# Latent attention of one layer with its up-projections moved from the keys and values to the queries and the outputs, in a two-block transformer kernel

## The reference

```python
c_kv = _rmsnorm(kv_raw, kv_norm_g)                      # (256 tokens, 256 latents)
q_lat = jnp.einsum('bqhd,hdc->bqhc', qb, w_uk)          # queries (head dim 128) into the latent space
logits = jnp.einsum('bqhc,bqkc->bqhk', q_lat, kv_sel) * DSA_HEAD_DIM ** -0.5   # minus slope * distance
p = jax.nn.softmax(logits, axis=-1)
o_lat = jnp.einsum('bqhk,bqkc->bqhc', p, kv_sel)
o = jnp.einsum('bqhc,hcd->bqhd', o_lat, w_uv)           # back to head dim 128
```

## Time and profile before

| what | value |
|---|---|
| median of 3 runs | 1394.24 us (1393.57 to 1398.60) |
| time of the profiled execution | 1398.6 us, its span 1396.9 us |
| mean granted TensorE clock | 0.978 of full |
| busy, share of the span | TensorE 88%, weight loads 66%, VectorE 77%, ScalarE 44%, GpSimd 21% |
| transfers | 416.63 MB, mean 298 GB/s |

### The profile page before, as it was taken

One profiled execution on the slowest core, in us unless ns is written; L12 is line 12 of the kernel. 1 busy time (PEld: TensorE's weight loads), 2 busy tenths in 40 slices (PEclk: granted clock), 3 DMA queues, 4 the chain that ended last, 5 costly groups with the idle time before them and its releaser, 6 DMA issues. The chain is left out here.

```text
span 1396.9 us, 19581 instructions
## 1 busy us (share of the span) xinstructions
PE 1233.3 (88%) x6990; PEld 923.0 (66%) x6990; DVE 1070.5 (77%) x2160; ACT 613.9 (44%) x1260; POOL 288.4 (21%) x278
## 2 busy tenths in 40 slices
PE   4999999998988877777877877778899999999998
PEld 3999999998933322333333322333599989999997
DVE  6897668778888777776777777776698968998656
ACT  4576365546244333233333333233553255554445
POOL 1000000001345534444444434442000000000000
PEclk8999999999999999999999999999999999999999
DMA  9946535554989999999999999999753444554460
GB/s 393 370 168 246 211 106 198 210 182 155 411 352 427 428 427 427 427 428 427 428 427 426 428 428 427 427 428 427 301 188 133 146 175 181 182 189 165 169 230 34
DMA packets 54911, 416.63 MB, mean 298 GB/s; under 512 B 6049, under 2 KB 6689, under 8 KB 8370
## 3 DMA queue, kind: packets, MB, share of 16 engines
q0 software_dynamic: 36864, 268.45, 45.7%
q1 hardware_dynamic: 17648, 146.78, 28.7%
q10 hardware_dynamic: 322, 0.36, 0.1%
HBM read 414.52 MB, written 1.05 MB: 298 GB/s over the span
## 5 line engine op out<-in xcount | busy, mean ns | idle before, releaser
L997 PE MATMUL ps<-arena 128*128 128x512 f32 x512 | 237.5, 610 | 63.1 <-ACT arena L1453 63.1
L997 PE MATMUL ps<-ring,arena 128*128 128x512 f32 x444 | 215.6, 637 | 46.0 <-ACT arena L1453 43.9
L997 PEld LDWEIGHTS ps<-arena 128*128 128x128 f32 x512 | 94.1, 192 | 204.5 <-ACT arena L1453 103.2
L2066 DVE CUSTOM_DVE_ANT_0 arena<-arena 128x1024 f32<-128x1024 f32 x128 | 151.9, 1224 | 100.5 <-DMA arena<-in_experts,rowid 95.6
L596 POOL DMA_INDIRECT arena<-in_experts,rowid x128 | 131.1, 1024 | 363.9 <-DVE rowid L2043 198.3
L997 PEld LDWEIGHTS ps<-ring,arena 128*128 128x128 f32 x444 | 87.8, 204 | 171.8 <-issue 98.9
L673 PE MATMUL ps<-h_hi,w_lo 128*128 128x256 f32 x704 | 197.3, 280 | 0.0
L672 PE MATMUL ps<-h_hi,w_hi 128*128 128x256 f32 x672 | 189.4, 282 | 1.0 <-DVE xT L2345 0.9
L1446 ACT ACTIVATE arena<-arena 128x2 f32<-128x2 f32 x126 | 25.6, 203 | 373.2 <-DVE arena L2066 373.0
L674 PE MATMUL ps<-h_lo,w_hi 128*128 128x256 f32 x672 | 187.8, 280 | 0.0
L596 POOL DMA_INDIRECT ring<-in_experts,rowid x112 | 130.5, 1165 | 140.4 <-PE ps L997 90.3
(11 more groups left out here) (362 smaller groups left out, 2532.0 us busy)
## 6 DMA issues: line engine op xcount, KB each, us to landing
ring<-in_early_w SPq DMA_DIRECT2D x47, 1024.0 KB, 4.9
arena<-in_ada_w SPq DMA_DIRECT2D x24, 1024.0 KB, 7.3
arena<-in_up_w SPq DMA_DIRECT2D x11, 2048.0 KB, 7.7
arena<-in_z_w SPq DMA_DIRECT2D x8, 2048.0 KB, 7.9
arena<-in_down_w SPq DMA_DIRECT2D x8, 1408.0 KB, 5.9
arena<-in_o_w SPq DMA_DIRECT2D x2, 2048.0 KB, 7.7
arena<-in_pg_w SPq DMA_DIRECT2D x2, 2048.0 KB, 8.3
arena<-in_experts,rowid POOLq DMA_INDIRECT x128
```

Of the source, the lines that this page charges most:

```text
L997: mm = pe.matmul(BK[4 + 2 * t + b], diag[:, j, :], rows[j][:, D + b * 512:D + (b + 1) * 512], start=first and j == 0, stop=last and j == ( ...
L2066: v.tensor_tensor_reduce(out=u, in0=u, in1=h2tok[:, t, :], scale=1.0, scalar=0.0, op0=ALU.mult, op1=ALU.add, accum_out=dots[:, even, j:j + ...
```

## The change

The weights w_uk are applied to the queries and w_uv to the mixed latents, as the reference's own lines have it. For each head TensorE now computes `head_query(h)` (two matmuls of 256 columns into BK[4], copied by ScalarE to qlat), `head_logits(h)` against the shared latents kvT with a contraction of 256 instead of 128, `head_mix(h)` against the latents for both halves of the 256 latent features (BK[7], copied by ScalarE to olat), and `head_out(h)` with w_uv into BK[6]. The mix needs the latents with tokens on the partitions: four transposes behind block gq 0, and a copy on VectorE (ckv_tok, 512 more values per partition). w_uk now comes in its given layout, in runs of 1 KB, instead of a host-made layout with 8 KB a partition.

```diff
                 if key == ("dq", 1):
                     sp.wait_ge(S("n1_ss"), KD)
-                    sp.dma_start(wuk, w["wuk_t"]).then_inc(S("dsa_in"), 16)
+                    sp.dma_start(wuk.rearrange("p a b -> p (a b)").rearrange("p (h c) -> p h c", c=LAT),
+                                 w["dsa_w_uk"][0].rearrange("h d c -> d h c")).then_inc(S("dsa_in"), 16)
...
             for b in range(4):
                 plain("gq", b)
+                if b == 0:
+                    pe.wait_ge(S("kv_h"), 1)
+                    for t in range(NT):
+                        for i in range(2):
+                            mm = pe.transpose(BK[7][:, t * LAT + i * P:t * LAT + (i + 1) * P],
+                                              kvT[:, i, t * P:(t + 1) * P], ident[:, :])
+                    mm.then_inc(S("ckv_mm"), 1)
...
             pe.wait_ge(S("gla_in"), 1)
+            pe.wait_ge(S("ckv_tok"), 1)
...
-            def head_kv(h):
-                for b in range(2):
-                    pe.matmul(BK[4][:, 0:T], wuk_h[:, h, b, :], kvT[:, b, :], start=b == 0, stop=b == 1)
-                for t in range(NT):
-                    for b in range(2):
-                        mm = pe.matmul(BK[4][:, T + t * P:T + (t + 1) * P], kvT[:, b, t * P:(t + 1) * P],
-                                       wuv[:, h, b, :], start=b == 0, stop=b == 1)
-                mm.then_inc(S("headkv_mm"), 1)
+            def head_query(h):
+                for b in range(2):
+                    mm = pe.matmul(BK[4][:, b * T:(b + 1) * T], wuk_h[:, h, b * P:(b + 1) * P], dqT[:, h, :],
+                                   start=True, stop=True)
+                mm.then_inc(S("qlat_mm"), 1)
             def head_logits(h):
-                pe.wait_ge(S("headkv"), h + 1)
+                pe.wait_ge(S("qlat"), h + 1)
                 for t in range(NT):
-                    mm = pe.matmul(BK[5][:, t * P:t * P + P * (t + 1)], dqT[:, h, t * P:(t + 1) * P],
-                                   headkv[:, h % 2, 0:P * (t + 1)], start=True, stop=True)
+                    for b in range(2):
+                        mm = pe.matmul(BK[5][:, t * P:t * P + P * (t + 1)], qlat[:, b, t * P:(t + 1) * P],
+                                       kvT[:, b, 0:P * (t + 1)], start=b == 0, stop=b == 1)
                 mm.then_inc(S("logit_mm"), 1)
             def head_turn(h):
                 pe.wait_ge(S("p_ready"), h + 1)
+                if h:
+                    pe.wait_ge(S("dsa_cp"), h)
...
             def head_mix(h):
                 pe.wait_ge(S("pT"), h + 1)
-                if h:
-                    pe.wait_ge(S("dsa_cp"), h)
-                for t in range(NT):
-                    for kt in range(t + 1):
-                        mm = pe.matmul(BK[7][:, t * P:(t + 1) * P],
-                                       headkv[:, h % 2, T + kt * P:T + (kt + 1) * P], pT[:, t + kt, :],
-                                       start=kt == 0, stop=kt == t)
+                for b in range(2):
+                    for t in range(NT):
+                        for kt in range(t + 1):
+                            mm = pe.matmul(BK[7][:, b * T + t * P:b * T + (t + 1) * P],
+                                           ckv_tok[:, kt, b * P:(b + 1) * P], pT[:, t + kt, :],
+                                           start=kt == 0, stop=kt == t)
+                mm.then_inc(S("olat_mm"), 1)
+            def head_out(h):
+                pe.wait_ge(S("olat"), h + 1)
+                for b in range(2):
+                    mm = pe.matmul(BK[6][:, 0:T], wuv[:, h, b, :], olat[:, b, :], start=b == 0, stop=b == 1)
                 mm.then_inc(S("dsa_mm"), 1)
...
-            head_kv(0)
+            head_query(0)
             for h in range(AH):
...
+                if h:
+                    head_out(h - 1)
                 if h + 1 < AH:
-                    head_kv(h + 1)
+                    head_query(h + 1)
                 plain(name, 2 * h % 8 + 1)
...
                 if b == 0:
                     head_mix(AH - 1)
+                if b == 1:
+                    head_out(AH - 1)
...
 -            def copy_kv(h):
-                act.wait_ge(S("headkv_mm"), h + 1)
-                act.activation(headkv[:, h % 2, :], BK[4], ACT.Copy).then_inc(S("headkv"), 1)
-            copy_kv(0)
+            def query(h):
+                act.wait_ge(S("qlat_mm"), h + 1)
+                act.activation(qlat.rearrange("p a b -> p (a b)"), BK[4], ACT.Copy).then_inc(S("qlat"), 1)
+            def mixed(h):
+                act.wait_ge(S("olat_mm"), h + 1)
+                act.activation(olat.rearrange("p a b -> p (a b)"), BK[7], ACT.Copy).then_inc(S("olat"), 1)
+            query(0)
...
                part()
+                if h:
+                    mixed(h - 1)
                 act.wait_ge(S("logits"), h + 1)
...
                 if h + 1 < AH:
-                    copy_kv(h + 1)
+                    query(h + 1)
...
+            mixed(AH - 1)
             act.wait_ge(S("taken_A"), taken[0])
             act.activation(za[:, :, :], za[:, :, :], ACT.Sigmoid).then_inc(S("gates"), 1)
...
             top_rounds(1, 3)
             rest()
+            v.wait_ge(S("ckv_mm"), 1)
+            link(v.tensor_copy(ckv_tok[:, :, :], BK[7].rearrange("p (a b) -> p a b", b=LAT)), "ckv_tok")
             top_rounds(1, 3)
...
             def head_copy(h):
                 v.wait_ge(S("dsa_mm"), h + 1)
-                link(v.tensor_copy(dsaT[:, h, :], BK[7][:, 0:T]), "dsa_cp")
+                link(v.tensor_copy(dsaT[:, h, :], BK[6][:, 0:T]), "dsa_cp")
```

More of the change, by code:

```diff
@@ L206, in split_count @@
     return n + 1 + (k // 2 if n == PARTED_EARLY else KD // 2 - 1)
-INPUTS = ["dsa_w_uv", "gla_w_gate_up"]
+INPUTS = ["dsa_w_uk", "dsa_w_uv", "gla_w_gate_up"]
 def two_blocks(nc, w, out):
@@ L332, in two_blocks @@
         decay = view(GH * 4)
+        ckv_tok = view(NT, LAT)
         madd = view(NT, T)
@@ L337, in two_blocks @@
         pT = view(3, P)
-        headkv = view(2, 2 * T)
+        qlat, olat = view(2, T), view(2, T)
         sm = view(8)
@@ L351, in two_blocks @@
         wuk = sq[:, :, :]
-        wuk_h = wuk.rearrange("p a b -> p (a b)").rearrange("p (h b d) -> p h b d", b=2, d=P)
         g_hi, g_lo = alias("g_hi", a_gr, KD, T), alias("g_lo", a_gT, KD, T)
@@ L860, in _, with head_logits @@
                 mm.then_inc(S("o_mm"), 1)
-            def head_kv(h):
+            wuk_h = wuk.rearrange("p a b -> p (a b)").rearrange("p (h c) -> p h c", c=LAT)
+            def head_query(h):
                 for b in range(2):
-                    pe.matmul(BK[4][:, 0:T], wuk_h[:, h, b, :], kvT[:, b, :], start=b == 0, stop=b == 1)
+                    mm = pe.matmul(BK[4][:, b * T:(b + 1) * T], wuk_h[:, h, b * P:(b + 1) * P], dqT[:, h, :],
+                                   start=True, stop=True)
+                mm.then_inc(S("qlat_mm"), 1)
+            def head_logits(h):
+                pe.wait_ge(S("qlat"), h + 1)
                 for t in range(NT):
                     for b in range(2):
-                        mm = pe.matmul(BK[4][:, T + t * P:T + (t + 1) * P], kvT[:, b, t * P:(t + 1) * P],
-                                       wuv[:, h, b, :], start=b == 0, stop=b == 1)
-                mm.then_inc(S("headkv_mm"), 1)
-            def head_logits(h):
-                pe.wait_ge(S("headkv"), h + 1)
-                for t in range(NT):
-                    mm = pe.matmul(BK[5][:, t * P:t * P + P * (t + 1)], dqT[:, h, t * P:(t + 1) * P],
-                                   headkv[:, h % 2, 0:P * (t + 1)], start=True, stop=True)
+                        mm = pe.matmul(BK[5][:, t * P:t * P + P * (t + 1)], qlat[:, b, t * P:(t + 1) * P],
+                                       kvT[:, b, 0:P * (t + 1)], start=b == 0, stop=b == 1)
                 mm.then_inc(S("logit_mm"), 1)
@@ L887, in head_mix @@
                 pe.wait_ge(S("pT"), h + 1)
-                if h:
-                    pe.wait_ge(S("dsa_cp"), h)
-                for t in range(NT):
-                    for kt in range(t + 1):
-                        mm = pe.matmul(BK[7][:, t * P:(t + 1) * P],
-                                       headkv[:, h % 2, T + kt * P:T + (kt + 1) * P], pT[:, t + kt, :],
-                                       start=kt == 0, stop=kt == t)
+                for b in range(2):
[9 more added lines that the diff above has]
+                    mm = pe.matmul(BK[6][:, 0:T], wuv[:, h, b, :], olat[:, b, :], start=b == 0, stop=b == 1)
                 mm.then_inc(S("dsa_mm"), 1)
             pe.wait_ge(S("dsa_in"), 32)
-            pe.wait_ge(S("kv_h"), 1)
-            head_kv(0)
+            head_query(0)
             for h in range(AH):
@@ L1326, in _ @@
                 act.activation(gT[:, 2 * h:2 * h + 2, :], oT[:, 2 * h:2 * h + 2, :], ACT.Square).then_inc(S("o_sq"), 1)
-            def copy_kv(h):
-                act.wait_ge(S("headkv_mm"), h + 1)
```

(7 more changed lines are left out.)

## The result

The changed kernel takes 1404.8 us (median of 6 runs, 1399.16 to 1410.55), the kernel before in the same session 1393.9 us (6 runs, 1393.12 to 1399.34). The ratio is 1.0076, 95% interval 1.0052 to 1.0099: slower by 10.6 us, between 7 and 14. Predicted were 1405.3 us and +11.1. In 33 further runs in other sessions, with no kernel before beside them, the changed kernel took 1400.19 to 1412.84 us, median 1405.8.

The account below looks back on a forecast made before the run. TensorE was taken to bound the heads, so added work moves everything behind it. 10.35 + 0.70 - 0.77 + 0.26 + 0.32 + 0.3 = 11.16, say +11.1 us on the median 1394.2: 1405.3 us, range 1400.5 to 1409.

Parts of the forecast that it names:

- the price is 0.431 us for each of 24 wide matmuls: In the eight heads, TensorE gains three 256-column f32 matmuls per head, priced by columns: +10.35 us.
- the rival in which the softmax chain sets the head: New matmuls fill gaps in the heads; only front and starts are paid: 1395.4 us; 7 in 100 together with a 1402.8 variant.
- the one in which a record costs a weight load: Every TensorE record costs a weight load whatever its columns: 48 x 0.101 = 4.8 us, total 1399.8; 3 in 100.
- the wait for pT: Before head_mix, TensorE's wait for the pT copy is covered by the longer logits: 7 x 0.11 = -0.77 us.
- Regrouping: First split matmul behind an f32 group starts its successor 0.09 us later; three more such changes, two behind head_out.
- The term of 0.70: Front and regrouping: four transposes behind gq 0, 0.43 us, plus 3 x 0.09 us of regrouping, +0.70 us.
- Starts of heads 0 and 1: Logits of heads 0 and 1 wait for ScalarE's copy as TensorE arrives earlier: +0.26 and +0.32 us.
- Room inside a head: Probabilities ready before head_turn needs them; head 5's margin grows from 0.56 to some 2.9 us; cost 0.
- Behind the last head: mixed(7) precedes the za sigmoid on ScalarE; three margins (ba 4, ba 6, bb 0) of 0.2 to 0.4 us; +0.3, bounds 0 and 1.5.
- the rival in which ScalarE's chain is late: Behind the last head, ScalarE's chain 1 us later misses all three meetings: up to +3 us, 1408; 12 in 100.
- VectorE's new copy: In front, one copy of 512 PSUM columns delays VectorE's next remainders: between 0 and 0.9 us, taken as 0.
- The w_uk transfer: 1 KB runs cost 0 to 0.7 us more transfer time, 120 us ahead of use; cost 0.

Follow-up runs that it names:

- the run with keys made: Changed kernel with each head's keys made as before and only the values left in the compressed space: 1402.72 us, ratio 1.0032 against the kernel before.
- the second profile: The changed kernel run once more, unchanged, timed against the kernel before: 1403.18 us, ratio 1.0075.
- the late copy: Changed kernel with ScalarE's last copy of the mixed latents moved behind the sigmoid of za and the weight split: 1404.92 us (one run).
- w_uk in rows: Changed kernel with w_uk brought in 8 KB a partition from a host-made layout instead of 1 KB runs: 1409.78 us (one run).
- the eightfold front: Changed kernel with its four front transposes of the compressed tokens run eight times over: 1406.8 us (one run).

## Why the prediction was right, step by step

- **TensorE sets the pace and the price is 0.431 us for each of 24 wide matmuls.** Shown: adding them alone costs the whole (ratio 1.0075), taking 23 of them away gives nearly all of it back (1.0017; 1.8 us of 9.9 stay between the marks). That rules out the rival in which the softmax chain sets the head (1395.4) and the one in which a record costs a weight load (4.8 us instead of 10.2).
- **The mis-sized term is the wait for pT.** Predicted 7 x 0.11 = 0.77 us gained, measured 1.29 - 1.10 = 0.19 a head, 1.3 us. The prediction counted the wait and left out the group behind it (+0.10 in the run with keys made) and the shape of the group ahead of a block. How the 0.19 divides between these isn't shown.
- **Regrouping.** The 0.09 us hold behind a group that ends in narrow matmuls. The two places behind `head_out` end in a wide one, and there it is 0.68 + 0.31 - 0.12 = 0.87 us for two wide matmuls of 0.86: next to nothing. The term of 0.70 was too high by 0.2 to 0.25.
- **Starts of heads 0 and 1.** Predicted +0.26 and +0.32; the wait of head 0's logits went from 0.69 to 0.91, +0.22. Head 1's begin 187.78 - 187.10 = 0.68 us behind the transposes instead of 0.33, +0.35 (the list of waits calls 0.20 of it a wait), and they take 1.42 us instead of 1.31: +0.46 for that head (10.73 against 10.27).
- **The sum and its luck.** With these it becomes 10.35 + 0.46 - 1.33 + 0.22 + 0.46 + 0.29 = 10.5 us, against 10.6 by the times (7 to 14) and 9.9 between the marks plus 0.4 to 0.5 for the front. The mechanism holds, and the predicted sum was about 0.6 us too high, which the times can't tell. That 1404.8 came within 0.5 us of 1405.3 is luck: runs of one kernel lie 6 to 12 us apart.
- **Room inside a head.** Predicted 2.9 us for the probabilities of head 5, measured 238.93 - 236.16 = 2.77. The copy of the head's output behind it has 1.66, which the prediction worked out only for a head without VectorE's work for the other branch (done at 6.9, needed at 10.0).
- **Behind the last head** +0.3, measured 0.29. The three margins of 0.2 to 0.4 us were missed twice, by 0.06 and 0.26 (0.06 and 0.07 in the second profile), and kept once. So the rival in which ScalarE's chain is late was right about the place and wrong about the size.
- **VectorE's new copy** takes 0.68 us in front, inside the 0 to 0.9 of the bounds, and nobody waits for it. **The w_uk transfer** is slower by 0.3 to 2.0 us, in the worst case more than the bound of 0.7, and hidden.
- **The gather stage** kept its length within the scatter: from the norm to the convolution 738.1 us before, 739.8 and 738.7 in two profiles after, 736.6 to 739.2 in the others.

## What to carry to other kernels

When the engine that sets the pace is busy without gaps, count its instructions before and after by shape and price them by the distance of starts in a run of the same shape: 24 x 0.431 gave the result to a microsecond, because the other terms, some 1.3 us gained and 1.4 us lost, nearly cancelled. A wait too short for the list of waits is found by comparing a group with the same group elsewhere, not by subtracting estimated lengths, and only where the blocks beside it run at the same pace; and a group that needs a fresh operand is best placed behind a block of other work. A margin in one head doesn't say how much delay the head can take, where the engine behind it has no gaps: look at its idle time over the whole stretch.

## What the runs showed of the hardware that I had not expected

The same block of split matmuls runs at one of two paces. In the last projection of the network (176 matmuls of each kind, the view by line) the profiles of one kernel, the changed one, show:

```profile
L1101 PE MATMUL ps<-f_hi,w_lo x176: 281/281/281, 1314.6 to 1376.4; 128*128 128x256 f32 x176
```
```profile
L1101 PE MATMUL ps<-f_hi,w_lo x176: 276/276/276, 1306.9 to 1366.4; 128*128 128x256 f32 x176
```

61.8 us in the first execution and 59.5 in the second, 0.117 and 0.113 us per matmul, with the granted clock at 1.00 in both. Of the thirteen profiles of this case four had the faster pace there and nine the slower, the kernel before among the nine. From the convolution to the last transfer it is 325.1 to 326.5 us in the four and 329.4 to 332.2 in the nine, so at least 2.9 us of what executions differ by goes with it.

Inside the heads the same two paces alternate within one execution, from block to block. In the changed kernel the place decides, once the heads are under way: in all five profiles of the changed kernel and its variants with full heads and VectorE as it was (the first, the second, the late copy, w_uk in rows, the eightfold front), from head 3 on, every block behind a mix runs at 0.113 to 0.114 us a matmul and every block behind a query (in head 7, behind the output) at 0.118. What sets the pace wasn't found. Besides, the granted clock between 960 and 1061 us is 0.97 in the profile before and 0.94 in the first one after. All this is why a single execution of this kernel can't tell 5 us, while the marks inside the heads repeat to 0.3 us.
